# A two-layer block on one core: five K groups in the first projections instead of four, the first two of two k tiles each

## The reference, cut to what matters

```python
c_act = jax.nn.silu(c)
mod = c_act @ w_ada[l] + b_ada[l]
sh1, sc1, gt1, sh2, sc2, gt2 = jnp.split(mod[:, None, :], 6, axis=-1)
h = rms_norm(x, g_pre_mix[l]) * (1.0 + sc1) + sh1
proj = h @ w_in[l]
u_glu, q, k, v, qi, ki, wi, gates = jnp.split(proj, [...], axis=-1)
y_conv = conv_branch(u_glu, ...)
y_attn = sparse_attn_branch(q, k, v, qi, ki, wi, w_attn_out[l])
mixed = (g_conv * y_conv + g_attn * y_attn) @ w_o[l]
x = x + gt1 * rms_norm(mixed, g_post_mix[l])
...
```

## Time and profile before

| what | value |
|---|---|
| median of 3 runs | 2722.52 us (2722.05 to 2723.39) |
| the profiled execution, its own time | 2721.6 us |
| its span in the profile | 2719.8 us |
| TensorE busy, share of the span | 95% |
| VectorE busy, share of the span | 63% |
| ScalarE busy, share of the span | 45% |
| mean granted TensorE clock | 0.985 of 2.4 GHz |

### The profile page before, as it was taken

How to read it: one execution, slowest core, us unless ns; L and a number is a source line. 1 busy time by engine, 2 the same in 40 slices (tenths; PEclk the granted TensorE clock), 3 DMA queues, 4 the chain that set the end, 5 groups by cost and what they waited for, 6 DMA issues and landing times.

```text
span 2719.8 us, 28903 instructions
## 1 busy us (share of the span) xinstructions
PE 2594.1 (95%) x11660; PEld 2115.9 (78%) x11660; DVE 1706.9 (63%) x2060; ACT 1212.6 (45%) x1605; POOL 3.4 (0%) x10
## 2 busy tenths in 40 slices
PE   4999988989989999999999999999999999999998
PEld 3777767777768888888888787778788888888886
DVE  6799799997766555555555554666554544445455
ACT  4545434335454444444444454554454444444443
POOL 0000000000000000000000000000000000000000
PEclk9999999999989999999999999999999999999999
DMA  9898565777755656665554544345545555555553
GB/s 357 317 346 319 201 204 199 249 258 264 276 190 188 227 204 229 237 244 203 218 207 179 186 171 166 143 146 180 200 159 196 186 187 204 197 186 190 190 192 124
DMA packets 80566, 579.29 MB, mean 213 GB/s; under 512 B 8964, under 2 KB 8964, under 8 KB 10544
## 3 DMA queue, kind: packets, MB, share of 16 engines
q1 hardware_dynamic: 78480, 564.82, 56.9%
q10 hardware_dynamic: 1440, 9.81, 0.9%
q0 software_dynamic: 512, 2.81, 0.3%
HBM read 573.73 MB, written 3.67 MB: 212 GB/s over the span
## 4 chain that ended last, share of the span: by engine, by line
PE 75%; DVE 10%; ACT 2%; issue 1%; ACTq 0%
PE bank L629 71%; DVE wlo L1425 3%; DVE cv L1420 3%; DVE raw L1435 1%; PE bank L593 1%; ACT whi L954 1%; DVE X L1420 1%; DVE SS L1420 0%; PE bank L789 0%; ACT SS L1302 0%; PE bank L874 0%; PE bank L661 0%; DVE STT L1594 0%; PE bank L731 0%; PE bank L894 0%
## 5 line engine op out<-in xcount | busy, mean ns | idle before, releaser
L1425 DVE TENSOR_TENSOR wlo<-raw,whi 128x1024 fp32r<-128x1024 f32 x882 | 1078.1, 1224 | 957.4 <-ACT whi L954 954.1
L954 ACT ACTIVATE whi<-raw 128x1024 fp32r<-128x1024 f32 x882 | 933.7, 1059 | 1382.1 <-PE bank L629 1305.0
L629 PE MATMUL bank<-whi,HTh 128*128 128x512 f32 x2560 | 710.5, 400 | 7.0 <-ACT HTh L954 5.8
L629 PE MATMUL bank<-wlo,HTh 128*128 128x512 f32 x2560 | 690.3, 392 | 14.5 <-DVE wlo L1425 14.5
L629 PE MATMUL bank<-whi,HTl 128*128 128x512 f32 x2560 | 690.2, 392 | 0.7 <-DVE HTl L1733 0.7
L629 PEld LDWEIGHTS bank<-wlo,HTh 128*128 128x128 f32 x2560 | 481.7, 189 | 120.5 <-DVE wlo L1425 18.5
L629 PEld LDWEIGHTS bank<-whi,HTl 128*128 128x128 f32 x2560 | 484.7, 189 | 105.1 <-DVE HTl L1733 1.2
L629 PEld LDWEIGHTS bank<-whi,HTh 128*128 128x128 f32 x2560 | 475.8, 191 | 112.8 <-issue 13.2
L1435 DVE CUSTOM_DVE_ANT_0 raw<-raw,GT,VECS 128x2048 f32<-128x2048 f32 x96 | 224.8, 2345 | 0.4 <-DMA raw<-in_w_ada 0.4
L629 PE MATMUL bank<-whi,ACTh 128*128 128x512 f32 x704 | 191.5, 394 | 0.0
L629 PE MATMUL bank<-wlo,ACTh 128*128 128x512 f32 x704 | 190.0, 392 | 0.0
(11 more groups left out here) (215 smaller groups left out, 1175.4 us busy)
## 6 DMA issues: line engine op xcount, KB each, us to landing
raw<-in_w_in SPq DMA_DIRECT2D x128, 1024.0 KB, 4.8
raw<-in_w_ada SPq DMA_DIRECT2D x96, 1024.0 KB, 5.2
raw<-in_w_gate SPq DMA_DIRECT2D x88, 1024.0 KB, 4.8
raw<-in_w_up SPq DMA_DIRECT2D x88, 1024.0 KB, 4.8
raw<-in_w_down SPq DMA_DIRECT2D x88, 1024.0 KB, 4.8
raw<-in_w_o SPq DMA_DIRECT2D x16, 1024.0 KB, 5.2
raw<-in_w_out SPq DMA_DIRECT2D x16, 1024.0 KB, 4.8
raw<-in_w_attn_out SPq DMA_DIRECT2D x8, 1024.0 KB, 4.8
```

The lines of the kernel that those rows point to most:

```text
L629: i = e.matmul(bank[2 * ch.st + t][:, :], (xl if ps == 1 else xh)[:, k, tk(t)], (lo if ps == 2 else hi)[:, j * 512:j * 512 + 512], start=c ...
L954: return e.activation(dst, src, ACT.Copy, scale=scale)
L1425: e.tensor_tensor(lo, src, r32(hi), S_).then_inc(lo_done, 1)
```

## The change: what it does

`KG` lists five K groups: two of two k tiles and three of four. A mm unit of a two-tile group is a *half unit*: half of the same 1 MB tile, 4 KB instead of 8 KB per partition, and it has one piece instead of two. So groups 0 and 1 have ten pieces each and groups 2 to 4 have 20; there are still 80 pieces, with the same matmuls. A chunk of groups 0 and 1 is one piece long. Four ada units come ahead of the first piece; group 0 has four more (after chunks 1, 3, 5 and 7), groups 1 to 4 eight each. Groups 1 to 4 are now added by VectorE. `first_h` of group 1 starts at step 7; those of groups 2 to 4 at the steps 17, 37 and 57 as before. The transposes of x use banks 4 and 5 in turn, one pair of tiles at each step. The core of the diff:

```diff
+LATE = 8
+KG = [(0, 2), (2, 2), (4, 4), (8, 4), (12, 4)]
...
     def mm(self, ch, src, off, kt, n, k0, share=0.0):
-        for half in range(2):
-            h = kt // 2
+        for half in range(1 if kt == 2 else 2):
+            h = 2 if kt == 2 else kt // 2
...
-    p.ada(early, 8)
-    for j in range(4):
+    p.ada(early, 4)
+    for g, (k0, kn) in enumerate(KG):
...
-                ch = p.chunk("part", (j, n), "h", "ACT" if j == 0 else "DVE", st=3 if n % 2 else 1)
-            p.mm(ch, "w_in", (c * 4 + j) * 128 * 2048, 4, 512, 4 * j)
-            p.ada(early if j < 3 else p.later, int(n < 8))
+                ch = p.chunk("part", (g, n), "h", "ACT" if g == 0 else "DVE", st=3 if n % 2 else 1)
+            p.mm(ch, "w_in", (c * 4 + k0 // 4) * 128 * 2048 + k0 % 4 * 512, kn, 512, k0)
+            p.ada(early if g < 4 else p.later, (n in (1, 3, 5, 7), n < 8, n < 8, n < 8, n < LATE)[g])
...
-            e.dma_start(flat(i)[:, 0:n], bass.AP(src.tensor, src.offset + u.off, [[n, 128], [1, n]])).then_inc(
+            e.dma_start(flat(i)[:, 0:n], bass.AP(src.tensor, src.offset + u.off, [[u.step, 128], [1, n]])).then_inc(
...
         def xts():
             for c in R(4, 16, 2):
-                if c > 4:
-                    w.wait_ge(*xt_act(c - 2))
-                xt(c, bank[5])
-                yield 2
+                if c > 6:
+                    w.wait_ge(*xt_act(c - 4))
+                xt(c, bank[4 + c // 2 % 2])
+                yield 1
...
-        for j, s in enumerate((17, 37, 57)):
+        for j, s in enumerate((7, 17, 37, 57)):
             lane.begin(s, first_h(j + 1))
...
-        for i in R(3):
+        for i in R(2):
             ada(i)
...
-        ada(3)
+        ada(2)
...
-        for i in R(4, 8):
-            ada(i)
-        mod(1, 0)
+        ada(3)
         for _ in first_h(0):
             pass
```

More of the change, by code:

```diff
@@ L13 @@
 AHEAD = 2
+LATE = 8
 ACTK = 24
+KG = [(0, 2), (2, 2), (4, 4), (8, 4), (12, 4)]
 FIRST = [10, 11, 0, 2, 1, 3, 8, 4, 5, 6]
-Unit = namedtuple("Unit", "kind src off kt n tag value")
+Unit = namedtuple("Unit", "kind src off kt n step tag value")
 Piece = namedtuple("Piece", "unit half kt n chunk ks")
@@ L68, in ada @@
             self.ada_at.setdefault(len(self.pieces), []).append(len(self.units))
-            self.units.append(Unit("ada", "w_ada", (tag[0] * 16 + tag[1]) * 128 * 2048, 4, 512, tag, self.ada_no[tag]))
+            self.units.append(Unit("ada", "w_ada", (tag[0] * 16 + tag[1]) * 128 * 2048, 4, 512, 2048, tag,
+                                   self.ada_no[tag]))
     def chunk(self, kind, j, x, by, st=None, first=True, last=True, apart=False, evictions=2):
@@ L90, in mm @@
             self.pieces.append(Piece(len(self.units), half, h, n, ch, range(k0 + half * h, k0 + half * h + h)))
-        self.units.append(Unit("mm", src, off, kt, n, None, None))
+        self.units.append(Unit("mm", src, off, kt, n, 2048 if kt == 2 else kt * n, None, None))
         self.owed += share
@@ L109, in make_plan @@
     p.later += [(w, c) for c in range(16) for w in (4, 3)]
-    p.ada(early, 8)
-    for j in range(4):
+    p.ada(early, 4)
+    for g, (k0, kn) in enumerate(KG):
         for n, c in enumerate(FIRST):
             if n == 0:
-                ch = p.chunk("first0", j, "h", "ACT", st=0, first=j == 0, last=j == 3)
+                ch = p.chunk("first0", g, "h", "ACT", st=0, first=g == 0, last=g == 4)
             else:
-                ch = p.chunk("part", (j, n), "h", "ACT" if j == 0 else "DVE", st=3 if n % 2 else 1)
-            p.mm(ch, "w_in", (c * 4 + j) * 128 * 2048, 4, 512, 4 * j)
-            p.ada(early if j < 3 else p.later, int(n < 8))
+                ch = p.chunk("part", (g, n), "h", "ACT" if g == 0 else "DVE", st=3 if n % 2 else 1)
+            p.mm(ch, "w_in", (c * 4 + k0 // 4) * 128 * 2048 + k0 % 4 * 512, kn, 512, k0)
+            p.ada(early if g < 4 else p.later, (n in (1, 3, 5, 7), n < 8, n < 8, n < 8, n < LATE)[g])
+    assert not early
     p.here("kiwi")
@@ L357, in build @@
     pro_pool = steps("pro_pool", ["zero", "ident"])
-    ada_mod = steps("ada_mod", [(w, j) for w in (1, 4) for j in R(4)])
+    ada_mod = steps("ada_mod", [(1, g) for g in R(5)] + [(4, j) for j in R(4)])
     gt_act = steps("gt_act", [(n, j, i) for n in R(2) for j in R(4) for i in R(4)])
@@ L364, in build @@
     xt_act = steps("xt_act", list(R(0, 16, 2)))
-    fh_dve = steps("fh_dve", [(k, c) for j in R(4) for k in ("h", "lo") for c in R(4 * j, 4 * j + 4)])
+    fh_dve = steps("fh_dve", [(k, c) for k0, kn in KG for k in ("h", "lo") for c in R(k0, k0 + kn)])
     fh_act = steps("fh_act", list(R(16)))
@@ L578, in sync @@
         w.wait_ge(out_done, n)
-    first_piece = {}
-    for p in R(NP - 1, -1, -1):
-        first_piece[P.pieces[p].unit] = p
+    pieces_to = {}
+    for p in R(NP):
+        pieces_to[P.pieces[p].unit] = p + 1
     def arrived(w, i):
@@ L1081, in xts @@
                 w.wait_ge(*xt_pe(c))
-                copy(pair(xT, c), bank[5][:, :]).then_inc(*xt_act.one(c))
-                yield 2
+                copy(pair(xT, c), bank[4 + c // 2 % 2][:, :]).then_inc(*xt_act.one(c))
+                yield 1
         def first_h(j):
-            for c in R(4 * j, 4 * j + 4):
+            for c in R(KG[j][0], sum(KG[j])):
                 w.wait_ge(*fh_dve("h", c))
@@ L1435, in ada, with mod @@
             e.tensor_tensor_reduce(src, src, CB[:, :], 1.0, vec("bada", which * 16 + c), M_, A_, out).then_inc(ada_done, 1)
-        def mod(which, j):
+        def mod(which, c, n, j):
             layer = which // 3
-            js = MA[:, layer, 4 * j:4 * j + 4]
-            w.wait_ge(*ada_of(which, 4 * j + 3))
-            stt(js, js, 1.0, vec("g1" if layer == 0 else "g2", 4 * j, 4), A_, M_).then_inc(*ada_mod.one(which, j))
+            js = MA[:, layer, c:c + n]
+            w.wait_ge(*ada_of(which, c + n - 1))
+            stt(js, js, 1.0, vec("g1" if layer == 0 else "g2", c, n), A_, M_).then_inc(*ada_mod.one(which, j))
         def mod_job(which, j):
-            mod(which, j)
+            mod(which, 4 * j, 4, j)
             yield 1
         def first_h(j):
-            if j:
-                mod(1, j)
+            mod(1, *KG[j], j)
             w.wait_ge(*ada_mod(1, j))
-            w.wait_ge(*ada_of(0, 4 * j + 3))
-            for c in R(4 * j, 4 * j + 4):
+            w.wait_ge(*ada_of(0, sum(KG[j]) - 1))
+            for c in R(KG[j][0], sum(KG[j])):
                 w.wait_ge(*xt_act(c // 2 * 2))
@@ L1491, in evict @@
                     w.wait_ge(*empty("part", (j - 1, n), t))
[L1492 removed]
+                    e.tensor_tensor(VV[:, t, 0:512] if (j, n) == (4, 6) else pt, B, pt, A_).then_inc(emptied["DVE"], 1)
                 elif ch.kind == "attn":
```

19 lines of the change are left out of this document (9 added, 10 removed).

## The result

| | before | changed |
|---|---|---|
| median of the runs, us | 2722.28 (4 runs, 2720.56 to 2723.39) | 2738.90 (4 runs, 2737.16 to 2741.51) |
| profiled execution, us | 2721.6 | 2738.6 |
| its span, us | 2719.8 | 2736.5 |

The ratio is 1.0062, with the 95% interval [1.0045, 1.0080]: slower, by 16.6 us in the medians and 17.0 in the profiled executions. The forecast was +10.7 (2733.2, range 2726 to 2740).

The account below looks back on a forecast made before the run. The prediction took TensorE, busy 95% of the span, as the bound. Group 1's +10.2 us (head's 3.6 gain taken off) plus 0.5 for loads gave +10.7 on 2721.6, 2732.3; with the median 0.9 higher, 2733.2 us, range 2726 to 2740.

Parts of the forecast that it names:

- The head: Before piece 0: four fewer ada units let piece 0 start at 37.76 instead of 41.37, -3.6 us.
- 0 to 2.8 given, 0 taken: Head: the second half of x might land earlier with fewer bytes queued, 0 to 2.8 us gain; 0 taken.
- the 1.8 us end: Head: the clock might stay up through the shorter gap before piece 0, 0 to 1.8 us gain; 0 taken.
- ScalarE empties after each piece; VectorE has ... hidden: Group 0, pieces 0 to 9: TensorE's work stays 33.43 us, VectorE's 22 us are hidden, piece 10 starts at 71.2.
- Group 1, VectorE's pace: Pieces 10 to 19: VectorE needs 4.60 us per chunk; piece 20 at 112.3 instead of 102.10, +10.2 us including the head's gain.
- VectorE waiting for raw units there: Group 1: sign that the forecast is wrong, pointing to the rival in which the stream becomes the bound.
- The loads: Group 1, steps 10 to 12: ada units up to 0.7 us late, at most three times; +0.5 us, ends 0 and 2.1.
- The clock in group 1: TensorE's gaps of 1.9 us may drop the clock, costing 0 to 3.5 us, mostly hidden behind VectorE; 0 taken.
- Behind piece 20: From piece 20 on nothing differs; the debt is not repaid and grows by 0 to 1 us.
- The backlog is absorbed: Rival: VectorE's group 1 work slides into slack behind piece 20, TensorE keeps its pace; 2717.1 us, chance 0.08.
- The head gives more: Rival: x 2.8 us earlier, clock up for 1.8, loads never late; 2728.1 us, chance 0.09 of within 0.2% of no change.
- The stream becomes the bound: Rival, group 1: a half unit holds the stream as long as a whole one, +7.3 us, 2740.5 us; chance 0.08.

Follow-up runs that it names:

- thin loads: Changed kernel with ada units 5 to 16 (the twelve of groups 0 and 1) loading 64 KB instead of 1 MB, VectorE's instructions kept: 2731.15 us, 1.0032.
- the second experiment: Changed kernel with full loads, VectorE's multiply and sum cut to 256 of 2048 elements for ada units 9 to 16: 2735.92 us, 1.0050.
- the run with split transfers: Kernel before, with each of the first 34 units of `w_in` loaded as two transfers of 512 KB with rows of 4 KB: 2724.74 us, 1.0010.
- the run with thin loads and short ada work: Changed kernel with thin loads, and VectorE's work on ada units 9 to 16 cut to 256 of 2048 numbers: 2727.46 us, 1.0020.
- the run with thin loads and ScalarE's emptyings: Changed kernel with thin loads, and group 1 emptied by ScalarE with overwriting copies instead of VectorE's additions: 2723.66 us, 1.0004.

## Why the prediction was right or wrong

**The head.** Forecast 37.76, measured 36.85. The order of the chain was as told. The timeline of the changed kernel:

```profile
23.88 0.63 ACT L967 ACTIVATE stg<-X 128x512 f32<-128x512 f32 x1 [2.41 <-DMA X<-in_x]
...
34.41 1.99 ACT L957 ACTIVATE whi<-raw 128x1024 fp32r<-128x1024 f32 x2
36.31 0.71 ACT L957 ACTIVATE HTh<-xT 128x256 fp32r<-128x256 f32 x2
...
36.85 1.17 PE L632 MATMUL bank<-whi,HTh 128*128 128x512 f32 x4 [1.60 <-ACT HTh L957]
37.86 1.07 PE L632 MATMUL bank<-whi,HTl 128*128 128x512 f32 x4
```

x landed 0.7 us earlier than in the earlier trace rows (0 to 2.8 given, 0 taken), but so did the first small tensor, and with thin loads, where the head is the same, x landed at 24.48 and piece 0 started at 37.46. So this is the spread between executions and no gain of the change, and 0 was right. The gap before piece 0 was 1.60 us instead of 5.76, and the clock stayed up through it, which is the 1.8 us end that was not taken. So the head was 0.9 + 1.8 = 2.7 us better than forecast, and 0.7 of it is chance.

**Group 0.** Its 33.43 us became 35.2 (36.85 to 72.04), though the clock should have made it 31.6: 3.6 us were lost, of which 2.8 stand in the timeline as waits of TensorE (2.26 before piece 3, 0.55 before piece 7) with late half units behind them. With thin loads the same group took 32.6 us (37.46 to 70.09). The step that failed is "ScalarE empties after each piece; VectorE has ... hidden", which looks at engines and takes the weights as landed.

```profile
48.12 1.06 ACT L957 ACTIVATE whi<-raw 128x1024 fp32r<-128x1024 f32 x1 [4.20 <-DMA raw<-in_w_in]
...
50.29 1.15 PE L632 MATMUL bank<-whi,HTh 128*128 128x512 f32 x4 [2.26 <-ACT PART L957]
```

**Group 1, VectorE's pace.** The 4.60 us per chunk are right to 0.1, and the run with thin loads came within 1 us of the forecast's piece 20. The order of waits (piece s for the emptying of chunk s-2) is right too: four waits on `PART` of 10.0 us. But VectorE "without gaps from 69 to 110" did not come, and "VectorE waiting for raw units there", which the prediction named as a sign of being wrong, did.

**The loads.** This is the term that was mis-sized: +0.5 taken, 2.1 as the upper end; measured between the changed kernel and the one with thin loads, 6.1 at piece 20 (117.42 - 111.32) and 7.8 over the run. It looked at steps 10 to 12 only, and beyond them compared rates, 341 GB/s wanted against 380 reached, which leaves out what was already owed when group 1 began. The change takes the lead that the stream had: four ada units fewer free their buffers ahead of piece 0, and the halves fill a buffer by half. As an estimate, at the 371 GB/s of the second experiment the missing 3.3 MB take 8.9 us, near the 7.8; that the sizes agree is no proof. Both halves of this cause stand in the diff (four ada units instead of eight; a buffer per half unit), so a count of the loads released before piece 0 would have pointed at it.

**The clock in group 1.** 0 taken, 0 to 3.5 given. Behind the gap of 4.97 us at piece 13 it fell, and that piece took 5.45 us (87.48 to 92.93); VectorE's step ended at 92.7, so it cost some 0.2. Behind the gaps of 1.62, 1.69 and 1.72 us it stayed at the full level of 2.4 GHz (1.17 and 1.08 us for four matmuls). The term is right. But the gaps were 0.2 to 0.3 us shorter than the 1.9 forecast, and in other runs gaps of 1.9 us dropped the clock (below), so some luck is in it.

```profile
87.48 2.04 PE L632 MATMUL bank<-whi,HTh 128*128 128x512 f32 x4 [4.97 <-DVE PART L1494]
89.32 1.91 PE L632 MATMUL bank<-whi,HTl 128*128 128x512 f32 x4
```

**Behind piece 20.** 0 to 1 us was forecast and 1.7 came (15.3 to 17.0). One place shows in the timeline, where TensorE's transposes waited 0.32 us before and wait 1.88 now:

```profile
253.94 0.63 PE L596 MATMUL bank<-ident,PART 128*128 128x128 f32 x4 [1.88 <-DVE PART L1494]
```

The rest is not settled. In the profiled executions of the experiments the total is between 2.3 us above and 1.7 below the shift at piece 20, except for the run with split transfers (+3.1), and single executions of the kernel before lie between 2718.35 and 2725.99, so 2 us may be no property of the change.

**The rivals.** "The backlog is absorbed" is refuted: piece 13 does wait for an emptying. "The head gives more" was right on the clock and not on x, and its gain was more than eaten by the stream. "The stream becomes the bound" was half right, in effect but not in mechanism: a half unit is cheap, and what was missing was a lead. Its 2740.5 lies near the result for another reason. The Trainium skill, "DMA: Bandwidth & Descriptors", section "Bandwidth", which asks for at least 1 MiB per transfer, points the same way as this rival; here 34 units in halves cost 2.7 us, and the stream reached 371 GB/s in group 1, where every second unit was a half.

The sum with the measured terms, at piece 20: 9.2 for VectorE's pace with the better head (111.32 - 102.10 in the run with thin loads; 10.2 was forecast) and 6.1 for the loads make the 15.3 of the table; 1.7 more came behind it. In the run with thin loads the head was 0.3 + 1.8 = 2.1 us better than forecast; half of it was gone by piece 10 (70.09 against 71.2), and the other 1.0 arrived at piece 20. Put in the prediction's terms, the forecast of +10.7 became +17.0 by 5.6 more for the loads and 1.7 behind piece 20, less 1.0 for the head. That the result still lies in the range, 1.1 us below its end, is in part luck: the loads went 4.0 us beyond their own upper end of 2.1, and what made room for them was the clock's end of 3.5, which did not come.

## What to carry to other kernels

Splitting the first K group buys an early start and pays with one more pass of emptyings; price that pass on the engine that does it, chunk by chunk. Then count the bytes that the ring of buffers can have let out when the first consumer starts: here fewer and smaller units ahead of it stopped the stream, and the debt showed up 10 to 60 us later, where it looks like a slow queue. When two limits lie this close together, taking the one in front away alone (VectorE's work) gained 2 or 3 us of 17 and seemed to prove it innocent; only the set of experiments, each alone and both together, gives each its price.

## What the runs showed of the hardware that was not expected

- A transfer of 512 KB with rows of 4 KB, queued among others, costs only 0.08 us more than its bytes (34 of them, 2.7 us [0.3, 5.2]).
- The clock does not answer to the length of a gap alone. It stayed up behind gaps of 1.60 to 1.73 us in every trace read here, but behind longer ones it did one or the other: up behind 1.98 and 2.26 us in the changed kernel, down behind 1.83 and 1.90 us in the run with thin loads and short ada work, and down behind 2.05 us before piece 0 in the run with thin loads and ScalarE's emptyings, where piece 0 then took 1.5 us more. A gap of 3.55 us in the same place of both kernels did both: the clock was down behind it in the kernel before (first row) and up in the changed one (second row). No run here separates what decides.

```profile
357.11 2.07 PE L629 MATMUL bank<-wlo,HTh 128*128 128x512 f32 x4 [3.55 <-DVE wlo L1425]
...
374.53 1.20 PE L632 MATMUL bank<-wlo,HTh 128*128 128x512 f32 x4 [3.55 <-DVE wlo L1428]
```
